# A data-dependent branch moved ahead of an expert loop, and one late weight transfer moved back in its queue

## The reference

```python
def hierarchical_moe(x, w_group, b_group, w_expert, b_expert, w_gate, w_up, w_down):
    g_logits = (x @ w_group).astype(jnp.float32) + b_group
    g_prob = jax.nn.softmax(g_logits, axis=-1)
    g_gate, g_idx = lax.top_k(g_prob, 1)
    ...
    e_gate, e_idx = lax.top_k(e_prob, TOP_K)
    ...
    for g in range(N_GROUPS):
        cw = (combine * group_mask[..., g:g + 1]).astype(x.dtype)
        hid = jax.nn.silu(jnp.einsum('bsd,edf->bsef', x, w_gate[g])) * jnp.einsum('bsd,edf->bsef', x, w_up[g])
        y = y + jnp.einsum('bsef,efd->bsd', hid * cw[..., None], w_down[g])
    return y

def reference(...):
    for l in range(DEPTH):
        mix = hybrid_mixer(x, w_in[l], w_out[l], rel_bias[l])
        x = layer_norm(DEEPNORM_ALPHA * x + mix, ln1_g[l], ln1_b[l])
        ffn = hierarchical_moe(x, ...)
        x = layer_norm(DEEPNORM_ALPHA * x + ffn, ln2_g[l], ln2_b[l])
    return x
```

## Time and profile before

| | us |
|---|---|
| median of 3 runs | 614.12 |
| lowest and highest | 609.05, 617.11 |
| profiled execution, its own time | 615.01 |
| its span in the trace | 613.3 |

### The profile page before, as it was taken

The page is one execution under the profiler, slowest core; times in us unless marked ns, Lnnn a source line. Parts: engine busy times, 40 slices in busy tenths (PEclk is TensorE's granted clock), DMA queues, the critical chain, the costliest instruction groups (busy, mean ns, idle before and its releaser), DMA issues.

```text
span 613.3 us, 7932 instructions
## 1 busy us (share of the span) xinstructions
PE 511.7 (83%) x3060; PEld 341.6 (56%) x3060; DVE 266.6 (43%) x434; ACT 159.2 (26%) x312; POOL 150.5 (25%) x129
## 2 busy tenths in 40 slices
PE   4999999999999977998528996788888887878692
PEld 4887776677667745886425553455444444544340
DVE  3300187779566645006522763332333231336167
ACT  4221445454544533225200111111111010111132
POOL 3433445535131310440010231111111111121000
PEclk9999999999999977999757998998888898999897
DMA  6433223932112133589940149999999999999743
GB/s 243 135 103 97 75 69 131 262 101 69 34 36 69 45 137 128 201 302 405 386 168 26 39 132 418 416 415 418 417 415 417 416 415 416 417 417 418 290 161 137
DMA packets 53239, 144.12 MB, mean 235 GB/s; under 512 B 11014, under 2 KB 27414, under 8 KB 45008
## 3 DMA queue, kind: packets, MB, share of 16 engines
q1 hardware_dynamic: 48160, 134.40, 57.0%
q0 software_dynamic: 5040, 9.18, 4.4%
HBM read 135.45 MB, written 16.27 MB: 247 GB/s over the span
## 4 chain that ended last, share of the span: by engine, by line
PE 39%; issue 8%; DMA 7%; DVE 6%; ACT 1%; SPq 0%; DVEq 0%; POOLq 0%
PE bank L1400 17%; PE bank L1427 8%; DMA gate_w<-in_w_gate 6%; PE bank L1388 2%; PE bank L1196 2%; PE bank L1198 2%; PE bank L1197 2%; PE bank L1402 2%; DMA xe<-h_rows,idx_all 1%; PE bank L1344 1%; PE bank L1413 1%; DVE hx L1158 1%; DVE xeT L1010 0%; DVE xeT L1014 0%; DVE hx L867 0%
## 5 line engine op out<-in xcount | busy, mean ns | idle before, releaser
L1400 PE MATMUL bank<-gate_w,xeT 128*64 128x256 f32 x512 | 133.1, 419 | 44.9 <-issue 42.1
L1402 PE MATMUL bank<-up_w,xeT 128*64 128x256 f32 x512 | 133.6, 420 | 0.0
L1400 PEld LDWEIGHTS bank<-gate_w,xeT 128*64 128x64 f32 x512 | 75.0, 152 | 82.4 <-issue 56.7
L478 POOL TENSOR_TENSOR w_lo<-raw,w_hi 128x1024 fp32r<-128x1024 f32 x32 | 80.6, 2520 | 131.4 <-ACT w_hi L586 131.4
L1402 PEld LDWEIGHTS bank<-up_w,xeT 128*64 128x64 f32 x512 | 74.9, 152 | 0.0
L1023 DVE TENSOR_TENSOR silu_hid<-silu_hid,bank 64x256 f32<-64x256 f32 x32 | 13.5, 423 | 136.4 <-ACT silu_hid L709 136.4
L1427 PE MATMUL bank<-down_w,hidT 128*64 128x512 f32 x256 | 61.4, 599 | 1.8 <-issue 1.8
L709 ACT ACTIVATE silu_hid<-bank 64x256 f32<-64x256 f32 x32 | 12.0, 376 | 186.1 <-PE bank L1402 186.1
L1196 PE MATMUL bank<-xT_hi,w_hi 128*128 128x512 f32 x128 | 53.6, 418 | 0.8 <-ACT values L605 0.8
L1198 PE MATMUL bank<-xT_lo,w_hi 128*128 128x512 f32 x128 | 50.7, 396 | 0.0
L1197 PE MATMUL bank<-xT_hi,w_lo 128*128 128x512 f32 x128 | 50.5, 395 | 0.0
(11 more groups left out here) (165 smaller groups left out, 795.4 us busy)
## 6 DMA issues: line engine op xcount, KB each, us to landing
gate_w<-in_w_gate SPq DMA_DIRECT2D x32, 1024.0 KB, 24.9
up_w<-in_w_up SPq DMA_DIRECT2D x32, 1024.0 KB, 24.6
down_w<-in_w_down SPq DMA_DIRECT2D x32, 1024.0 KB, 24.1
raw<-in_w_in SPq DMA_DIRECT2D x24, 512.0 KB, 3.9
expert_rows<-xe SPq DMA_DIRECT2D x1, 4096.0 KB, 15.1
raw<-in_w_out SPq DMA_DIRECT2D x8, 512.0 KB, 3.4
hx<-in_x SPq DMA_DIRECT2D x4, 512.0 KB, 5.2
h_rows<-hx SPq DMA_DIRECT2D x4, 512.0 KB, 11.4
```

The costliest lines, as they stand in the source:

```text
L478: nc.gpsimd.tensor_tensor(w_lo[:, slot, :], raw[:, slot, :], w_hi[:, slot, :].bitcast(F32), ALU.subtract).then_inc(s_lo, 1)
L1400: nc.tensor.matmul(GATE[h], xeT[:, m % 2, c, half(h)], gate_w[r][:, c, :], start=(c == 0), stop=(c == KD - 1))
L1402: mm = nc.tensor.matmul(UP[h], xeT[:, m % 2, c, half(h)], up_w[r][:, c, :], start=(c == 0), stop=(c == KD - 1))
```

## The change

The branch of all five engines moves ahead of the expert loop, and the number of passes is worked out inside `fill_slots(0)`, between its first operation and its wait for PE. On POOL it stands after the first gather, on PE before the first transpose. The loop then covers all 32 experts on PE, ACT and DVE, with no wait for `s_all`; SP waits for the scatters themselves. On SP the down matrix of slot seven, with its wait for `s_scaled`, is issued after the matrices of expert 9 instead of before those of expert 7. In the last part PE takes the rows of the last two experts first, one tile ahead, and the scattered rows second. ACT loads the square root's table by an explicit preload ahead of each norm. The body of the branch is changed so that it can run first (it restores the ring's first two slots, the ranks, the indices and the first gather).

```diff
@@ SP
             sp.wait_ge(s_idx, 1)
-            expert_matrix(6, 6, 0)
-            expert_matrix(6, 6, 1)
-            sp.wait_ge(s_scaled, T)
-            expert_matrix(6, 6, 2)
-            for e in range(RING, E):
...
             sp.wait_ge(s_passes, 1)
             with sp.If(n_passes > 1):
...
             with sp.Else():
                 sp.nop(nofuse=True)
-            sp.wait_ge(s_all, 1)
+            expert_matrix(6, 6, 0)
+            expert_matrix(6, 6, 1)
+            for e in range(RING, E):
+                sp.wait_ge(s_gu, e - RING + 1)
+                expert_matrix(e % RING, e, 0)
+                expert_matrix(e % RING, e, 1)
+                sp.wait_ge(s_dn, e - RING + 1)
+                expert_matrix(e % RING, e, 2)
+                if e == RING + 2:
+                    sp.wait_ge(s_scaled, T)
+                    expert_matrix(6, 6, 2)
+            sp.wait_ge(s_dn, E - 4)
...
+            for h in range(2):
+                sp.wait_ge(s_put[h], 16 * LAST)
             for t in range(T):
                 sp.dma_start(first_y[:, t, :], y_v[:, 0, t, :]).then_inc(s_first[t], 16)
@@ POOL
-            for m in range(3):
-                get(m)
...
+            get(0)
             pool.wait_ge(s_passes, 1)
             with pool.If(n_passes > 1):
...
-            pool.sem_inc(s_all, 1)
+            for m in range(1, 3):
+                get(m)
+            pool.wait_ge(s_zero, 16)
+            pool.wait_ge(s_odd, 1)
+            for e in range(2 * LAST):
+                if e % 2 == 1 and (e + 5) // 2 < MOE_PAIRS:
+                    get((e + 5) // 2)
+                put(e)
@@ ACT
+            nc.scalar.preload_act_table_set("sqrt_and_others")
             centre_and_root(0)
...
-                if e >= 2 * LAST:
-                    act.wait_ge(s_all, 1)
-                elif e >= 2:
+                if e >= 2:
                     act.wait_ge(s_put[h], 16 * (e // 2))
...
+                if e == E - 1:
+                    nc.scalar.preload_act_table_set("sqrt_and_others")
@@ DVE, in fill_slots
+                if isinstance(ps, int):
+                    count_passes()
                 dve.wait_ge(s_slotted, ps + 1)
@@ PE
-            for e in range(2 * LAST, E):
-                gate_up(e)
-                turn_hidden(e)
+            turn_x(0)
+            gate_up(0)
+            turn_x(1)
+            turn_hidden(0)
+            for e in range(E):
+                if e + 1 < E:
+                    gate_up(e + 1)
...
                 down(e)
+                if e + 1 < E:
+                    turn_hidden(e + 1)
...
+            def last_rows(t):
...
+                    nc.tensor.matmul(bank[:, b + j, :], place_T[:, t, :], y_rows[:, j * 512:(j + 1) * 512],
+                                     start=True, stop=False)
+            def second_rows(t):
...
+            last_rows(0)
             for t in range(T):
-                last_sums(t)
+                if t + 1 < T:
+                    last_rows(t + 1)
+                second_rows(t)
```

More of the change, by code:

```diff
@@ L530, in put @@
                     oob_is_err=False).then_inc(s_put[h], 16)
-            for m in range(3):
-                get(m)
-            pool.wait_ge(s_zero, 16)
-            pool.wait_ge(s_odd, 1)
-            for e in range(2 * LAST):
-                if e % 2 == 1 and (e + 5) // 2 < MOE_PAIRS:
-                    get((e + 5) // 2)
-                put(e)
-            for h in range(2):
-                pool.wait_ge(s_put[h], 16 * LAST)
+            get(0)
             pool.wait_ge(s_passes, 1)
-            n_passes = pool.value_load(passes_i[0:1, 0:1], min_val=0, max_val=S // SLOTS)
+            n_passes = pool.value_load(passes_i[0:1, 0:1], min_val=1, max_val=S // SLOTS)
             with pool.If(n_passes > 1):
+                pool.wait_ge(s_get, 16)
+                pool.wait_ge(s_zero, 16)
                 with pool.Fori(1, n_passes) as ps:
@@ L1080, in last_places @@
                 then_place(ins)
[L1082 to L1103 removed]
+            n_passes = dve.value_load(passes_i[0:1, 0:1], min_val=1, max_val=S // SLOTS)
             with dve.If(n_passes > 1):
@@ L1136, in _ @@
                             nc.vector.tensor_copy(y_rows[half(h), D // 2:], DN[h][1]).then_inc(x_yd, 1)
+                dve.wait_ge(x_go, n_passes)
+                dve.nop(nofuse=True)
+                with dve.Fori(1, n_passes) as ps:
+                    nc.vector.tensor_scalar(rank[:, :, :], rank[:, :, :], float(SLOTS), None, ALU.add
+                                            ).then_inc(s_lower, 1)
+                    dve.wait_ge(s_lower, n_passes + ps - 1)
+                    dve.nop(nofuse=True)
+                fill_slots(n_passes)
             with dve.Else():
                 dve.nop(nofuse=True)
-            for e in range(2 * LAST, E):
-                product(e)
-                turned_out(e)
-                second_half_out(e)
+            turned_tokens(0)
+            turned_tokens(1)
+            product(0)
+            turned_out(0)
+            for e in range(E):
+                if e + 1 < E:
+                    product(e + 1)
+                if e % 2 == 1 and (e + 3) // 2 < MOE_PAIRS:
+                    turned_tokens((e + 3) // 2)
+                second_half_out(e)
+                if e + 1 < E:
+                    turned_out(e + 1)
+                if e < T:
+                    scaled_rows(e)
+                if e == E - 5:
+                    last_places()
+                if e == E - 4:
+                    dve.wait_ge(s_turned, 1)
+                    nc.vector.tensor_copy(place_T[:, :, :].rearrange("p t n -> p (t n)"), bank[:, 6, :]
+                                          ).then_inc(s_placeT, 1)
+            assert placed[0] == PLACED
             dve.wait_ge(s_scaled, T)
@@ L1431, in _ @@
             pe.wait_ge(s_passes, 1)
-            turn_x(0)
-            gate_up(0)
-            turn_x(1)
-            turn_hidden(0)
-            for e in range(2 * LAST):
-                if e + 1 < 2 * LAST:
-                    gate_up(e + 1)
-                if e % 2 == 1 and (e + 3) // 2 < MOE_PAIRS:
-                    turn_x((e + 3) // 2)
-                if e == E - 4:
-                    pe.wait_ge(s_place, PLACED)
-                    pe.wait_ge(s_xeTs, MOE_PAIRS)
-                    for t in range(T):
-                        mm = nc.tensor.transpose(bank[:, 6, t * P:(t + 1) * P],
-                                                 place[:, t, :, :].rearrange("p h s -> p (h s)"), ident[:, :])
-                    mm.then_inc(s_turned, 1)
-                down(e)
-                if e + 1 < 2 * LAST:
-                    turn_hidden(e + 1)
-            n_passes = pe.value_load(passes_i[0:1, 0:1], min_val=0, max_val=S // SLOTS)
+            n_passes = pe.value_load(passes_i[0:1, 0:1], min_val=1, max_val=S // SLOTS)
             with pe.If(n_passes > 1):
```

114 lines of the change are left out of this document (59 added, 55 removed).

## The result

| | before | after |
|---|---|---|
| median, us | 611.59 | 588.87 |
| lowest and highest, us | 608.45, 617.11 | 587.86, 597.52 |
| ratio after to before | | 0.9614, interval 0.9513 to 0.9714 |
| profiled execution, us | 615.01 | 588.45 |
| its span, us | 613.3 | 586.7 |

The forecast was 587 us, the range 580 to 598. The kernel is faster by 23 us. But the sum of the terms was 27.4, and the experiments put only the first term on firm ground. Three later sets of runs, on three chips, gave the kernel before medians of 609.3, 610.1 and 610.4, so the base of the forecast (614.12, from three runs) was some 4 us too high, and the terms behind the first were too large by about as much. Two errors cancelled, and that the total came within 2 us is in part luck.

The account below looks back on a forecast made before the run. The expert stage was held bound by the weight stream, which stood nearly still until SP's wait for the last `scaled_rows` ended. Gains of 22.7 + 3.4 + 1 + 0.3 = 27.4 us gave 587 us, range 580 to 598.

Parts of the forecast that it names:

- the base of the forecast: Whole kernel before: profiled execution of 615.01 us, with the median of the runs taken as 0.9 lower.
- the terms behind the first: Gains forecast besides the moved down matrix: loop end 3.4 us, branch 0, first gather 1, square root's table 0.3.
- The late down matrix, -22.7: SP's weight stream: nine matrices of 2.52 us move before 362 us, and all 22.7 us reach the end.
- The end of the loop, -3.4: Last experts: one loop ends 5.8 us earlier, the new order of last sums takes back 2.4, net 3.4.
- the case that the forecast named, as an aside: Last expert: if `gate_up` 31 starts at the low clock (5.2 us), only 1.7 us of the loop-end gain are left.
- The paragraph on the loads: Last sums: `first_y` loads issued near 578, first in 3.8 us later, at 582 to 583; PE needs it at 586.
- The branch, 0: Ahead of the expert loop: its cost of up to 4.2 us on PE hides in the 8.99 us first-gather wait.
- The first gather, -1: Before the first transpose: expert 6's weights are issued later, so the gather has the DMA engines alone; 1 us gained.
- The bound of 3: First gather: its 7.5 us can't get shorter by more than 3, since PE's branch ends near 313.
- The table, -0.3: First norm: preloading the square root's table wins at most the 0.2 to 0.35 us gap on DVE; 0.3 counted.
- the first two rivals: Expert loop: early weights delay gathers, 590 to 595 us, chance 0.13; gathers become the period, 621 us, chance 0.03.
- The third: Expert loop: the prefetch brings only 5 to 10 us of the 22.7, so 601 to 608 us; chance 0.06.

## Why the prediction was right or wrong

**The late down matrix, -22.7: right.** The two pairs of kernels with and without the move differ by 23.2 and 22.6 in B, and in time by 22.5 and some 26 us. The line of thought held at each step: nine matrices between 326.7 and 351, no PE wait for weights before expert 17, period 12.4 up to there. (A slip that changes nothing: the page's slice 24 begins at 368 us, not at 362; the full rate does begin at 362.)

**The end of the loop, -3.4: not borne out.** Measured in the pair of traces it is -2.7, near the forecast by luck, as the second trace of the kernel before is 5 us shorter in this stretch, and against it the change costs 2.3 to 3.6; the ratios show nothing either way. The gap of 4.17, taken as a property of the branch, is one draw out of 0.8 to 5.2, and the low clock behind it cost 1.6 us more; with both the forecast compared an unlucky end. One loop doesn't shorten what follows the weights: looking ahead puts a `gate_up` that waits in front of a `down` that could run, and behind the pause PE fell to the low clock in four of seven traces (the case that the forecast named, as an aside). The sums were close: 0.8 + 3 x 1.73 is 6.0, not 6.1, and 6.4 was measured. The paragraph on the loads has 2.6 us from `down` 29 to its scatter, where the rows give 1.6 (569.21 - 567.65); the issue came 7.1 us behind the end of `down` 29 (547.73, 554.85), where it had 7. But it counted 3.8 us for the first load, while DVE needs those of two tiles, 8.2 us after the issue (554.85 to 563.0), so little of its slack was there.

**The branch, 0: right for its own instructions.** In the new place PE's wait ends with the gather in every trace, and where the gather came 4.8 us sooner the branch was over by then too. The Trainium skill ("Runtime: NRT & Kernel Launch", Instruction fetch mechanics) says that a taken branch out of the fetched window stalls for a fetch. Gaps of 0.8 to 5.2 us at one branch, and none without it, go with that. The forecast took the 4.17 as the worst of sharing the DMA engines. That isn't so: the DMA share was 0.98 in the gap of 0.81, 0.93 in that of 4.17 and 0.71 in that of 5.19. What sets the length stays open.

**The first gather, -1: wrong, +1.5.** I had expected it to have the engines to itself because the weights are issued later. The branch delays SP by only 1.0 us (from 0.85 ahead of the gather to 0.15 behind it), so they are issued right behind it, and behind it the gather takes 9.1 us, right ahead 7.6. The bound of 3 was slightly tight: alone the gather takes 3.3 less than in the kernel before. What these 1.5 us cost at the end is at most that; 0.4 to 1.0 shows in B.

**The table, -0.3: as said.** The table load is at 272.49, ahead of the first square, and costs nothing. DVE's first norm, from its first sum to the start of its last normalising step, takes 8.93 us (278.17 to 287.10) where it took 9.22 (279.55 to 288.77): 0.29 less.

**The rivals.** From a gather's issue to PE's next transpose there are 10.5 us in each pair from 344 us until expert 17, and PE never waits; the landings read directly are 8.2 us in the median. So the first two rivals didn't come, though the forecast's 6 was too low. The third didn't either, since B is shorter by all nine matrices. But the first gather shows that a gather can be held up by weights. The Trainium skill ("DMA: Bandwidth & Descriptors", Queues, rings and completion order) says that an engine takes turns between its queues by the packet. For the later gathers the trace agrees (8.2 us beside weights that need 26). For the first it agrees less: beside two matrices, 5.04 us at full rate, the gather lost 3.3 and 4.8.

**The base.** The forecast took 615.01 for an execution 0.9 above the median. It was 5 above the medians of 41 later runs, and as much lies between the two traces of that kernel in the stretch that I priced from it (C, 41.0 and 36.1).

## What to carry to other kernels

A transfer that has to wait for a late consumer must not stand in a queue ahead of transfers that don't: move it back to where its slot is next needed, and read the gain as the count of transfers that pass it, as long as the stream leads at the end. Where an engine waits for data at the end of a loop, work that needs no new data belongs in front of the wait, so a lookahead can cost in the last turns (1.5 to 4.5 us in C here, though no median shows it, and what it gains in the middle wasn't measured). A gap that stands in one trace is one draw: take a second trace of the kernel before pricing a stretch of 5 us.

## What the runs showed that I had not expected

The cost of jumping over a branch body that isn't run varies sixfold between executions of the same code (0.81, 4.17 and 5.19 us), and the low clock behind the two long gaps adds 1.6 and 2.5 us in the next `gate_up`. A gather of 0.30 MB needs 4.3 us alone, 7.6 with 2.1 MB issued up to 0.84 us ahead of it, 9.1 with the same issued up to 0.52 us behind it, and 8.2 beside a stream at full rate.
